# Block one's order rearranged around its attention and norms, and block two's residual stream kept normed instead of scaled by alpha

## What is computed

```python
# block one
y = concat([rmsnorm(merge(ya), g_out_dil), rmsnorm(merge(yb), g_out_moba)])
h = h + y @ w_out
h = h + memory_cross_attention(rmsnorm(h, g_cross), rmsnorm(mem, g_mem), w_q, w_kv, w_o)
h = h + conv_ffn(rmsnorm(h, g_ffn), ...)
# block two
def post_norm(x, y): return layer_norm(ALPHA * x + y)         # layer_norm has EPS beside the variance
xl = post_norm(xl, 0.5 * g1 * swiglu(modulate(xl, sh1, sc1), w_in, w_out))
xl = post_norm(xl, g2 * mixer(modulate(xl, sh2, sc2)))
xl = post_norm(xl, 0.5 * g3 * swiglu(modulate(xl, sh3, sc3), w_in, w_out))
```

## Time and profile before

| | us |
|---|---|
| median of 3 runs | 2323.25 (2321.92 to 2324.7) |
| profiled execution | 2322.09 |
| its span on the core | 2320.3 |
| TensorE busy | 2218.7 |
| VectorE, ScalarE, GpSimd busy | 1420.0, 976.4, 755.2 |

### The profile page before, as it was taken

One profiled execution on the slowest core, in us unless ns is written; L12 is line 12 of the kernel. 1 busy time (PEld: TensorE's weight loads), 2 busy tenths in 40 slices (PEclk: granted clock), 3 DMA queues, 4 the chain that ended last, 5 costly groups with the idle time before them and its releaser, 6 DMA issues.

```text
span 2320.3 us, 34014 instructions
## 1 busy us (share of the span) xinstructions
PE 2218.7 (96%) x13148; PEld 1906.8 (82%) x13148; DVE 1420.0 (61%) x2103; ACT 976.4 (42%) x1585; POOL 755.2 (33%) x378
## 2 busy tenths in 40 slices
PE   6989989999999998988999999999999999989997
PEld 6978889998888876866788888878888878878997
DVE  3644454548887667757777766579756474447335
ACT  4655446543222336455442222253223254455443
POOL 3424325452222233521233322234222224214543
PEclk9999999999999999999999999999999999999999
DMA  7426535455464331120334443234454362214553
GB/s 256 171 95 263 224 128 191 159 178 198 165 227 168 132 118 51 53 73 1 127 109 150 168 172 119 99 136 152 169 205 158 104 147 92 73 55 140 177 180 105
DMA packets 79406, 329.98 MB, mean 142 GB/s; under 512 B 18912, under 2 KB 29280, under 8 KB 55696
## 3 DMA queue, kind: packets, MB, share of 16 engines
q1 hardware_dynamic: 79248, 327.81, 40.6%
HBM read 326.70 MB, written 1.08 MB: 141 GB/s over the span
## 4 chain that ended last, share of the span: by engine, by line
PE 82%; DVE 7%; issue 5%; ACT 5%; DMA 1%; POOL 0%; DVEq 0%; SPq 0%; ACTq 0%; POOLq 0%
PE ps L526 26%; PE ps L528 25%; PE ps L527 25%; PE ps L711 1%; ACT WH L1041 1%; PE ps L742 1%; DMA WF<-in_w 1%; PE ps L702 1%; DVE TMP L1621 1%; DVE WL L1545 1%; PE ps L687 1%; PE ps L721 1%; DVE AR L1958 0%; DVE TMP L1648 0%; DVE TMP L1560 0%
## 5 line engine op out<-in xcount | busy, mean ns | idle before, releaser
L2174 POOL TENSOR_TENSOR WL<-WF,WH 128x1024 fp32r<-128x1024 f32 (+2 forms) x253 | 598.0, 2364 | 1342.3 <-ACT WH L1041 1341.7
L526 PE MATMUL ps<-Hh,WH 128*128 128x256 f32 (+1 forms) x2536 | 860.3, 339 | 33.9 <-DVE WL L1545 10.8
L527 PE MATMUL ps<-Hl,WH 128*128 128x256 f32 (+1 forms) x2536 | 854.9, 337 | 0.0
L528 PE MATMUL ps<-Hh,WL 128*128 128x256 f32 (+1 forms) x2536 | 854.6, 337 | 0.0
L1041 ACT CAST WH<-WF 128x1024 fp32r<-128x1024 f32 (+3 forms) x507 | 466.3, 957 | 304.8 <-PE ps L528 296.6
L526 PEld LDWEIGHTS ps<-Hh,WH 128*128 128x128 f32 x2536 | 484.8, 191 | 98.9 <-issue 45.6
L528 PEld LDWEIGHTS ps<-Hh,WL 128*128 128x128 f32 x2536 | 484.8, 191 | 49.6
L527 PEld LDWEIGHTS ps<-Hl,WH 128*128 128x128 f32 x2536 | 485.1, 191 | 49.1 <-issue 0.2
L1621 DVE CUSTOM_DVE_ANT_0 TMP<-AR 128x1024 f32<-128x1024 f32 x216 | 416.0, 1965 | 8.6 <-DMA AR<-in_ada 7.3
L1545 DVE TENSOR_TENSOR WL<-WF,WH 128x1024 fp32r<-128x1024 f32 (+2 forms) x254 | 312.8, 1232 | 136.8 <-ACT WH L1041 136.3
L526 PE MATMUL ps<-HIDh,WH 128*128 128x512 f32 (+1 forms) x880 | 307.7, 350 | 3.8 <-DVE WL L1545 3.8
(11 more groups left out here) (226 smaller groups left out, 2089.2 us busy)
## 6 DMA issues: line engine op xcount, KB each, us to landing
WF<-in_w SPq DMA_DIRECT2D x170, 1024.0 KB, 4.8
AR<-in_ada SPq DMA_DIRECT2D x120, 512.0 KB, 5.7
WF<-in_w SPq DMA_DIRECT2D x80, 704.0 KB, 4.1
AR<-in_piece SPq DMA_DIRECT2D x12, 1024.0 KB, 8.3
AR<-bias_rows SPq DMA_DIRECT2D x3, 1024.0 KB, 12.8
AR<-in_rpb SPq DMA_DIRECT2D x12, 256.0 KB, 6.6
AR<-in_cond SPq DMA_DIRECT2D x2, 1024.0 KB, 7.6
X<-in_x SPq DMA_DIRECT2D x2, 512.0 KB, 4.6
```

The source lines that it names most:

```text
L526: e.matmul(out, lh, rh, start=first, stop=False, skip_group_check=parts)
L527: e.matmul(out, lh, rl, start=False, stop=False, skip_group_check=parts)
L528: return e.matmul(out, ll, rh, start=False, stop=end, skip_group_check=parts)
L2174: e.tensor_tensor(l[:, k0:k1, :], src[:, k0:k1, :], h[:, k0:k1, :].bitcast(F32), ALU.subtract).then_inc(*up("p_lo", ("lo", i, 1)))
```

## The change

- Startup: idle matmuls before and behind the statistics of x. Half 1 of the first chunk gets its high part from GpSimd and its low part from VectorE. The two Silu activations on the conditioning vector, and the logarithm's table, move from behind the first norm into the first step of ka. Six sums over the memory's squares move from GpSimd to VectorE.
- First attention: qb, kb, vb stand one to a step in steps 0 to 5, km and vm[0..2] one to every second step from 6 to 18. vm[3] stands behind wout in the plan and is run between the cross statistics and qm; the four qm chunks run one after another, no longer two in a pair.
- Norm of y: the modulation pieces run before the second statistics; y is scaled in place in X, and wout[1]'s casts stand between its high parts.
- FFN f0: the casts of f0_gu[1] move behind the last square and into the norm's casts; `pe_ada_turn(5)` moves from behind the pair to behind gu[2].
- Block two: the gates are divided by ALPHA and the norm's constant by ALPHA squared, so that X needs no factor alpha. VectorE writes X * root back into X (tile 0 last), ScalarE modulates from X, and the residual operations of GpSimd and ScalarE are gone.

```diff
-    for c in range(4):
+    for c in range(3):
...
+    out.append(("vm", k8, [("w_kv", rng(1024 + 256 * 3, 256))]))
...
-    SECOND = {CH[name][j] for name, j in (("qm", 1), ("f0_gu", 1), ("f10_gu", 1), ("e_lr", 0), ("f20_gu", 1),
+    SECOND = {CH[name][j] for name, j in (("f0_gu", 1), ("f10_gu", 1), ("e_lr", 0), ("f20_gu", 1),
...
-    work1 = [("qb", 0), ("qb", 1), ("kb", 0), ("kb", 1), ("vb", 0), ("vb", 1)]
-    for i in range(4):
-        work1.insert(2 * i, ("mem", i))
-    work1 += [("km", i) for i in range(4)] + [("vm", i) for i in range(4)]
-    work1 = spread(work1, 10) + [[] for _ in range(6)]
+    work1 = [[] for _ in range(19)]
+    for i, items in ((0, [("mem", 0), ("qb", 0)]), (1, [("mem", 1), ("qb", 1)]), (2, [("mem", 2), ("kb", 0)]), (3, [("mem", 3), ("kb", 1)]),
+                     (4, [("vb", 0)]), (5, [("vb", 1)]), (6, [("km", 0)]), (8, [("km", 1)]), (10, [("km", 2)]), (12, [("km", 3)]),
+                     (14, [("vm", 0)]), (16, [("vm", 1)]), (18, [("vm", 2)])):
+        work1[i] = items
...
                 if name == "att1" and end in (3, 7):
-                    pe_stat(e, ("y", end // 4), S, [(HT[10], ("ysum", end // 4)), (HT[11 + end % 2], ("ysq", end))])
...
+                    pe_stat(e, ("y", end // 4), S, [(HT[10], ("ysum", end // 4)), (HT[11 + end % 2], ("ysq", end))])
...
                 pe_pair(e, of, *[(CH[name + "_gu"][n], T, gate_tiles(name, n)) for n in range(2)])
-                pe_ada_turn(e, 5)
...
+                if n == 2:
+                    pe_ada_turn(e, 5)
...
         au = acts(hu, "uh", "ul")
+        zeros = SC[:, :, :].rearrange("p k c -> p (k c)")
+        pe_idle(e, "load", 7, zeros[:, 0:P], zeros, ("zeros",))
...
+        pe_idle(e, "x", 5, ident, X[:, 0, lat])
...
         ac = acts(hu, "ch0", "cl0")
-        pe_pair(e, ac, *[(CH["qm"][c], S, [(("qm", j), [("qm", j)]) for j in (2 * c, 2 * c + 1)]) for c in range(2)])
-        for c in range(2, 4):
-            pe_lin(e, CH["qm"][c], ac, S, [(("qm", j), [("qm", j)]) for j in (2 * c, 2 * c + 1)])
+        pe_work1(e, "vm", 3)
+        for c in range(4):
+            pe_lin(e, CH["qm"][c], ac, S, [(("qm", j), [("qm", j)]) for j in (2 * c, 2 * c + 1)], fresh=c == 0)
...
+    def act_y_high(e, k):
+        e.wait_ge(*at(("yt", k)))
+        e.wait_ge(*at(("end", CH["vb"][1])))
+        e.copy(hu[k][0], X[:, k, con]).then_inc(*up("h_hi", ("yh", k)))
...
-        if k >= 4:
-            e.wait_ge(*at(("yt", k - 4)))
-            e.wait_ge(*at(("end", CH["vb"][1])))
-            e.copy(hu[k - 4][0], HT[13]).then_inc(*up("h_hi", ("yh", k - 4)))
+        if k > 4:
+            act_y_high(e, k - 5)
...
-                    e.mul(X[:, n, con], X[:, n, con], ALPHA).then_inc(*up("ctx_x", ("cxx", n)))
...
-        e.activation(r, t, ACT.Ln, bias=eps).then_inc(*up("ln", (st, "ln")))
+        e.activation(r, t, ACT.Ln, bias=cst("eps_post")).then_inc(*up("ln", (st, "ln")))
...
                 up_, sh = MOD[:, l, 8 * (g + 1) + k, r:r + 1], MOD[:, l, 8 * g + k, r:r + 1]
-                e.wait_ge(*at((st, "mt", k, 0 if k else r)))
+                e.wait_ge(*at((st, "res", k) if k else (st, "mt", r)))
...
-                    e.activation(t[:, c], t[:, c], ACT.Identity, bias=sh, scale=up_).then_inc(*up("mod_t", (st, "mt2", k, r)))
+                    if k >= 3:
+                        e.wait_ge(*at((st + "l", k - 3)))
+                    e.activation(t[:, c], X[:, k, c], ACT.Identity, bias=sh, scale=up_).then_inc(*up("mod_t", (st, "mt2", k, r)))
...
-        e.mul(SQ[:, 0:T], STAT[0][:, 0:T], ALPHA).then_inc(*up("mean", (before, "up")))
...
-        act_split(e, WIDE[0])
+        act_half(e, WIDE[0], 0)
...
-        act_highs(e, range(KT), [HT[7 + k % 6] for k in range(KT)], "uh", "ut")
-        e.wait_ge(*at(("vec",)))
-        e.wait_ge(*at(("zeros",)))
-        e.activation(SC[:, :, 0], vec("c", 0, 8), ACT.Silu)
-        e.activation(SC[:, :, 1], vec("c_ctx", 0, 8), ACT.Silu).then_inc(*up("silu", ("silu",)))
-        act_logs(e)
+        slots = [HT[7 + k % 6] for k in range(KT)]
+        act_highs(e, range(KT), slots, "uh", "ut")
...
+            if c == 0:
+                e.wait_ge(*at(("vec",)))
+                e.wait_ge(*at(("zeros",)))
+                e.activation(SC[:, :, 0], vec("c", 0, 8), ACT.Silu)
+                e.activation(SC[:, :, 1], vec("c_ctx", 0, 8), ACT.Silu).then_inc(*up("silu", ("silu",)))
+                act_logs(e)
...
         act_attention(e, "att1", units1, 64 ** -0.5, work1, act_work1, act_y)
-        act_highs(e, range(4, 8), {k: HT[k - 4] for k in range(4, 8)}, "yh", "yt")
-        act_logs(e)
+        act_y_high(e, 3)
+        for k in (4, 6):
+            act_highs(e, (k, k + 1), {j: HT[j - 4] for j in range(4, 8)}, "yh", "yt")
+            act_half(e, CH["wout"][1], k // 2 - 2)
...
-            act_splits(e, CH["wout"][c])
+            if c:
+                act_splits(e, CH["wout"][c])
...
-                    act_half(e, CH["qm"][1], 0)
+                    act_half(e, CH["qm"][0], 0)
...
-        act_half(e, CH["qm"][1], 1)
+            if c == 1:
+                act_logs(e)
+        act_half(e, CH["qm"][0], 1)
...
+        for t in range(2):
+            act_evict(e, VM[:, t, 768:1024], ("vm", 3, t)).then_inc(*up("a_evict", ("vm", 3, t)))
...
             for j in (2 * c, 2 * c + 1):
-                if j == 7:
-                    act_half(e, CH["f0_gu"][1], 0)
...
+        act_half(e, CH["f0_gu"][1], 0)
+        act_root(e, "ffn", S, D, 0)
+        slots = [HT[8 + k % 6] for k in range(KT)]
+        act_highs(e, range(3), slots, "fh", "ft")
...
-        act_root(e, "ffn", S, D, 0)
-        act_highs(e, range(KT), [HT[8 + k % 6] for k in range(KT)], "fh", "ft")
+        act_highs(e, range(3, KT), slots, "fh", "ft")
...
-    def dve_split(e, i):
+    def dve_split(e, i, q=0):
...
-        k0, k1 = halves(i)[0]
-        e.wait_ge(*at(("hi", i, 0)))
+        k0, k1 = halves(i)[q]
+        e.wait_ge(*at(("hi", i, q)))
...
-            *up("w_lo", ("lo", i, 0)))
+            *up("w_lo", ("lo", i, q)))
...
-        if g != 3:
-            e.tensor_scalar(m[:, 16:24, :], m[:, 16:24, :], 0.5, None, ALU.mult)
+        e.tensor_scalar(m[:, 16:24, :], m[:, 16:24, :], (1.0 if g == 3 else 0.5) / ALPHA, None, ALU.mult)
...
+        if k > 4:
+            dve_low(e, hu[k - 5][1], X[:, k - 5, con], hu[k - 5][0], ("yh", k - 5), ("yl", k - 5))
...
-            dve_scaled(e, HT[13], X[:, k - 4, con], vec("g_out", k - 4), STAT[0][:, 0:S], ("yt", k - 4), ("root", ("y", 0)),
-                       ("yl", k - 5) if k > 4 else ("ml", 7))
-            dve_low(e, hu[k - 4][1], HT[13], hu[k - 4][0], ("yh", k - 4), ("yl", k - 4))
+            dve_scaled(e, X[:, k - 4, con], X[:, k - 4, con], vec("g_out", k - 4), STAT[0][:, 0:S], ("yt", k - 4), ("root", ("y", 0)))
...
             if k < KT:
-                t = TMP[k % 3]
+                t = TMP[0]
...
-                if k >= 3:
-                    e.wait_ge(*at((st + "l", k - 3)))
...
-                    e.tensor_tensor(t[:, 0:T], X[:, k, 0:T], root[:, 0:T], ALU.mult).then_inc(*up("scaled", (st, "mt", k, 0)))
+                    e.tensor_tensor(X[:, k, 0:T], X[:, k, 0:T], root[:, 0:T], ALU.mult).then_inc(*up("scaled", (st, "res", k)))
...
-                                               in1=root[:, c], op0=ALU.mult, op1=ALU.mult).then_inc(*up("scaled", (st, "mt", k, r)))
+                                               in1=root[:, c], op0=ALU.mult, op1=ALU.mult).then_inc(*up("scaled", (st, "mt", r)))
...
+        e.tensor_tensor(X[:, 0, 0:T], X[:, 0, 0:T], root[:, 0:T], ALU.mult).then_inc(*up("scaled", (st, "res", 0)))
...
-                    dve_gated(e, st, l, g + 2, T, n, (st, "d", h, n), (st, "x0", n), (st, "res", n), ("mod", l, g),
-                              *([("cxx", n)] if st == "f10" else []))
+                    dve_gated(e, st, l, g + 2, T, n, (st, "d", h, n), (st, "x0", n), ("mod", l, g),
+                              *([("xf", n), ("ctx",)] if st == "f10" else [(st, "res", n)]))
...
         dve_split(e, WIDE[0])
+        dve_split(e, WIDE[0], 1)
...
             dve_qk(e, 4 + 2 * c + 1)
+        for k in range(1, 7):
+            e.wait_ge(*at(("msq", k)))
+            e.wait_ge(*at(("msum", k - 1) if k > 1 else ("msq", 0)))
+            e.tensor_tensor(HT[0], HT[0], HT[k], ALU.add).then_inc(*up("d_sum", ("msum", k)))
...
+        dve_low(e, hu[3][1], X[:, 3, con], hu[3][0], ("yh", 3), ("yl", 3))
...
-        dve_pieces(e, *PIECES["y"])
...
+            if c == 0:
+                dve_pieces(e, *PIECES["y"])
...
-        dve_split(e, CH["qm"][1])
+        dve_split(e, CH["qm"][0])
...
-    def pool_residual(e, st, before, k, T):
...
-        e.wait_ge(*at((before, "up")))
-        e.wait_ge(*at((st, "mt", k, 0 if k else T // S - 1)))
-        e.tensor_tensor(X[:, k, 0:T], X[:, k, 0:T], SQ[:, 0:T], ALU.mult).then_inc(*up("p_x", (st, "res", k)))
...
-    def pool_swiglu(e, st, before, T):
+    def pool_swiglu(e, st, T):
...
```

(55 more changed lines are left out.)

## The result

The changed kernel takes 2294.8 us (median of 4 runs, 2292.7 to 2296.7) where the one before takes 2323.5 beside it: a ratio of 0.9877, 95% interval 0.9860 to 0.9894, 28.7 us less. The prediction said 2290 within 2278 to 2302.

The account below looks back on a forecast made before the run. TensorE's stream of small matmuls bounds the kernel, so only its idle or half-clock time can go: 5.0 + 13.7 + 1.7 + 0.5 + 8.0 + 4.0 = 32.9 off 2322.1 gives 2289.2, 2290 on the median, range 2278 to 2302.

Parts of the forecast that it names:

- Startup, 5.0: Start to the bias rows and on to 54.8: table loads gone and clock back, +5.0 us (3.0 to 6.5).
- a DMA chain of fixed length: Behind the bias rows: three transfers of 8.47 us, then weights; said to carry the whole startup shift to 54.8.
- Attention, 13.7: End of the first attention: seven single products close the holes, +13.7 us (9 to 16.4); prediction wrong if under 9.
- the serial rival: Attention steps: a pair's softmax starts only after splits and evictions, 11.8 us a step instead of 8.6; 2312 us, chance 0.08.
- about 1 us at the statistics of the first half: End of the attention, norm of y: a wait said to stay, as little as the trace's short waits.
- The tail at wout: Behind the attention: second root, scaling, casts and low part take 4.5 us, wout's tiles cover 2.9, leaving 1.6.
- Cross norm, 1.7: Cross norm: vm3 fills TensorE's 1.67 us wait for the norm's last low part, +1.7 us.
- FFN entry, 8.5: Block one's FFN: moving the modulation's turn removes the bank wait, +8.0 us (2 to 9.5), and +0.5 for the entry.
- elsewhere: FFN entry: 1.6 us of the 6.6 us TensorE idles, outside the 5.03 us wait for issue.
- Block two, 4.0: GLA entry: GpSimd passes no longer stretch VectorE or delay a split, 3 us plus 1 of clock, +4.0 us (-0.5 to 9).
- the modulation's products at 1.2 us: Sign in block two: custom instructions at 1.2 us; a modulation product was said to take 3.41 beside passes, 1.22 without.
- The trailing product on VectorE: Block two: one added VectorE product per norm, 0.69 us, said to be hidden; tightest case 3.5 us over five norms.

Follow-up runs that it names:

- the added matmuls: Changed kernel with y's scaling behind the next step's bias addition, the bias table's third part copied, and three idle matmuls in mix0: 2288.4 us.
- block two alone: Kernel before with only the block two half of the change, block one as before: 2318.4 us, ratio 0.9977 (0.9967 to 0.9987).

## Why the prediction was right, and where it wasn't

- **Startup, 5.0 against 4.3.** Right in its one cause, the table loads, and in giving the idle matmuls and the split cast nothing. At the bias rows the shift is the forecast's: their product starts 4.7 us earlier (4.6 forecast). I let it run whole through "a DMA chain of fixed length". But the tables' reads go out only 4.1 us earlier, and the cast of qb[0] starts 3.8 earlier, while TensorE reaches its first scores 6.6 us earlier: a wait of 2.0 to 4.6 us opened at qb[0].
- **Attention, 13.7 against 8.3** (10.0 less 1.7 in wout). This is the mis-sized term. It lies under the 9 us below which the prediction called itself wrong, so by its own sign it failed here, although the total came out inside the range. The steps run at 8.4 us from pair to pair (forecast 8.6), so the serial rival is out. The failed step is "about 1 us at the statistics of the first half". I priced the root of the second half with one table load and the root of the first not at all. It has two loads, 3.5 us in all, on a ScalarE that is busy for 5.7 of a step's 8.4 us, and the scaling held by GpSimd comes on top: 0.7 + 2.57 us of waits and, in this trace, 3 us from the 6.1 at half clock. The Trainium skill's page "ScalarE: Activation LUTs" (Table sets: the hidden batching unit) states that one set holds both exp and ln, so that a root could do with one load or, between exponentials, none; no run here shows it. The tail at wout (1.00 + 0.34 in its tiles, 0.57 before) was forecast at 1.6.
- **Cross norm, 1.7 against 1.6**, as worked out.
- **FFN entry, 8.5 against 10.2** with the norm ahead. The place of the turn was the cause, shown by undoing it; that it acts through its bank fits the wait's end beside the reduction. The 1.58 us wait came back with it, which I had counted as "elsewhere". Of the 9.1 us in f0, 1.5 are the fall of the clock that comes and goes: without it f0 and the entry give 8.7 against 8.5, so most of the excess over the forecast is chance. I kept 2 us back for holes behind; none over 0.5 us opened.
- **Block two, 4.0 against 4.1 by the runs, but not where I put it.** I placed 4 us in the GLA entry. The mechanism there was right, VectorE's instructions stretched by passes, and the wait did shrink by 4.2, but mix0 kept 0.4 of it at most: the rest went to a later wait for VectorE and to a fall of the clock. What is left is 0.9 us in each inner FFN; the other 2 us of the 4.1 can't be placed in a stage, since the clock's steps of 1.5 us hide them. That the sum is near 4.0 all the same is luck. The prediction also wanted the modulation's products at 1.2 us; the mean of that line went from 1965 ns to 1883, and the longest is still 3.42. I had misread the row of 3.41 us at 1183.12 as one beside passes:

```profile
1182.97 2.48 POOL L2174 TENSOR_TENSOR WL<-WF,WH 128x1024 fp32r<-128x1024 f32 x1 [1.91 <-ACT WH L1041]
1185.40 4.50 POOL L2187 TENSOR_TENSOR X<-X,SQ 128x512 f32<-128x512 f32 x2
```

(GpSimd, kernel before.) For 2.3 us of its 3.41 the product ran beside a split, which the change keeps. Of the 92 products over 1.5 us before the change, 14 ran beside passes alone; 77 over 1.5 us are left, all beside splits. The trailing product on VectorE shows in no wait, as forecast.

The sum was off by 4 us, with the attention 5.4 us short and the FFN entry 1.7 over. The answer is inside its range although the account of the attention failed: the range had room for the miss, and a part of it was made up elsewhere by chance.

## What to carry to other kernels

When a stall is a bank or buffer waited for by position in a rotation, look for the small tile that took it and whose reader stands far behind: moving that tile by one product was a quarter of this gain (7 of 28.7 us). When an edit closes the end of a chain, price every step that enters the newly full stretch, roots with their table loads above all, against the slack per step of the engine that runs them. And follow a shortened wait to the end of its stage before counting it: mix0 kept 0.4 of 4.2 us at most.

## What the runs showed of the hardware that was not expected

A wait of the same length, at the same instruction, is followed by a fall of the clock in one execution and not in another. Behind the wait of 2.8 us for issue at the end of f0, the changed kernel shows:

```profile
497.00:505.00 8.00, 6.92 (x31) 5.75 (x31) 6.04 (x6) 3.99 (x6) 3.60 (x2) 1.00 0.55 197
```

and the one in which ScalarE casts the first chunk whole:

```profile
497.00:505.00 8.00, 8.00 (x23) 6.34 (x24) 7.06 (x8) 3.00 (x4) 2.50 (x2) 0.62 0.53 197
```

f10 takes 348.2 us in eight of the twelve experiments' traces and 349.8 to 351.0 in the other four; in those four mix0 is 282.4 to 282.6 instead of 284.1 to 284.6 (287.2 with the added matmuls), so a step can be given back in the next stage. With the turn in its new place f0 takes 222.6 to 222.8 or 224.3; mix1 up to its statistics takes 206.9 to 207.1 or 208.4 to 208.6: steps of 1.5 us. The trace of the kernel before had such falls in f0 (block two alone, with the same block one, has f0 at 229.2 and not 231.9), so part of the 9.1 us there is that. In this kernel, with some twenty waits of 1 to 4 us, single traces differ by this much with no cause in the code, and a stage's gain under 2 us is to be trusted only where the clock of both stretches is the same.

A GpSimd instruction holds a VectorE instruction with two SBUF inputs in some cases and not in others. In the changed kernel's trace the scaling of 128x256 (line 1576) runs 48 times. Three of these began while a GpSimd operation with two inputs was running, and took 2.24, 0.96 and 0.60 us: each ended 0.28 us after that operation. One that had begun 0.2 us before a split took 0.48, and so did the rest. GpSimd's cast with one input held nothing: in all eleven traces with it, a low part on VectorE inside it took 1.22 to 1.23 us, its time without GpSimd. For such operations the prediction's sentence on any GpSimd instruction that reads SBUF, quoted there from the Trainium skill's page "SBUF — State Buffer" (Who interferes with whom), is not borne out.
